# Reordering the ends of the layer normalisations in a two-layer hybrid decoder kernel: transposes in four banks, the layers written out, the last step in halves, angle tables later, the store in parts

## The chip, the core and the metric

The kernel runs on one core of a Trainium2 chip (trn2). The metric is the device time of one execution in microseconds, as the median of several runs. The engines are named as in the profile: PE is TensorE (PEld its weight loads), DVE is VectorE, ACT is ScalarE, POOL is GpSimd, SP is the engine that issues most DMAs. A name with a small q at its end (DVEq, SPq) is an engine's queue: its branches, register instructions and DMA issues.

## The reference

Two post-norm decoder layers over 256 tokens of width 1024, in float32. What matters here is where the normalised stream `x` is made and who reads it:

```python
h = layer_norm(x, ln_in_g, ln_in_b)
for l in range(DEPTH):                       # DEPTH = 2
    # token mixing: one input projection, MLA and NSA attention, gates, output projection
    c_q, c_kv, k_r, n_q, n_kv, n_gate, m_gate = split(h @ w_in[l])
    ...
    h = layer_norm(ALPHA * h + mixed, ln1_g[l], ln1_b[l])
    # channel mixing: PEER retrieval over 128*128 single-neuron experts
    q = h @ peer_w_query[l]; ...; a = h @ expert_u.T (dense in the kernel); ...
    h = layer_norm(ALPHA * h + peer(h), ln2_g[l], ln2_b[l])
```

So the stream is normalised five times in a run: once for the input, and twice in each layer. The rotary embeddings need the cosine and sine of position times frequency, one small table for the whole run.

## The kernel before

**Tiles.** The tokens are two groups `tt` = 0, 1 of 128 rows; `xs` holds the stream, 128 partitions x 2 x 1024. All weights stream from memory as 512 KB tiles of 128 x 1024 into a ring of four slots (`raw`). Each is split in two parts whose sum is the full number: ACT writes the high part (`split_hi`, L443), DVE writes what is left (`split_lo`, L701), and every product is three matmuls (low x high, high x low, high x high: L1206 to L1208 where the result is wanted transposed, L1217 where tokens are rows). A slot is free again when PE has used its tile, and only then SP issues the next load into it (L367). Tile n+3 is split while tile n is multiplied (`AHEAD` = 3). A layer has 68 front tiles (8 for the latent projections, 52 more up to the output projection, 8 for the PEER query), then 128 tiles of expert keys (the "u" stage, L1515) and, after a stage that builds the gates from one-hot rows (L1539), 128 tiles of expert values (the "v" stage, L1554).

**A normalisation.** DVE does for each token group, one after the other: add the wide sum out of PSUM (L1021), statistics (two of L715, then L717), the variance (L721), subtract the mean and multiply by the gain (L723), and, when POOL has made the inverse root (L408), the last step (L728), which multiplies by it and adds the bias. L728 is one instruction of 128 x 1024; it adds 1 to the semaphore `x_ready`.

**After it.** The next matmuls want `x` transposed and split as well. PE transposes 128 x 128 blocks, four to a PSUM bank (L1235), in the order g = 0..3: g = 0, 1 are the halves of token group 0, g = 2, 3 those of group 1. The PSUM tensor `tr` has two banks, so g = 2 must wait until the low part of g = 0 has been read out (`tr_free`, L1194). For each g ACT writes the high part (L476) and then DVE the low part (L779). When DVE has done all four (`xT_written`), PE starts on the first tile. PE, ACT and DVE each follow a fixed order of instructions. On ACT the high parts come after the splits of three weight tiles; on DVE, at the first layer's start and at the second's, the low part of weight tile 0 comes first, then the four low parts of `x`, then those of tiles 1 and 2. After the first normalisation of a layer the low part of the first query tile is put between L723 and L728 of token group 1 (`meanwhile`).

**The start.** DVE first computes the angles (L736 to L751, 13 instructions, on a tile `ang` that overlays the latents), then the input normalisation, then copies the sines and cosines that ACT has made (L465, L466) into the tables (L761 to L768), and then enters the loop over layers.

**The loop.** On each engine the two layers are one loop of hardware instructions (`Fori(0, DEPTH)`, L369, L412, L468, L772, L1228) around inner loops; addresses and the values that waits compare with are computed from the loop register.

**The end.** When both groups are ready SP stores all of `xs`, 1 MB, with one DMA (L375).

## Time and profile before

| | before |
|---|---|
| median of 3 runs | 2387.64 us (2386.96 to 2390.41) |
| the profiled execution | 2391.61 us, of which 2390.0 us are the span |
| PE busy | 2191.5 us (92%) |
| PE weight load busy | 1976.3 us (83%) |
| DVE busy | 1579.1 us (66%) |
| ACT busy | 1190.1 us (50%) |
| DMA | 353 MB, mean 148 GB/s |

The busy shares are averages over the stages. In 40 equal slices of the span (one digit is the busy share in tenths, a 9 is 90% or more; PEclk is the clock that TensorE was granted, in tenths of its 2.4 GHz):

```profile
PE   6989989999996699999988898999999967999997
DVE  5546567777769955555556466577777698555555
PEclk9989999999999999999989899999999999999999
```

The slices where PE falls below 9 are the start, the attention stages, the gate stages (slices 13 and 33), the places where one normalisation ends and the next product begins, and the end.

### The profile page before, as it was taken

To read this page: it belongs to the slowest core of one execution; us is meant where nothing else is said; L and a number is where in the kernel's file an instruction comes from. 1 tells how busy PE (TensorE), PEld (TensorE's weight loads), DVE (VectorE), ACT (ScalarE), POOL (GpSimd) and SP (SyncE) were. 2 spreads that over 40 slices of the span, in tenths; PEclk is the share of its full clock that TensorE was granted. 3 is DMA by queue.
4 is the path that set the end of the run, shared out by engine and by line. 5 is a ranking of instruction groups with operands and counts; after the bars stand their busy time and mean duration, and the time that the engine had idled before them with its cause. 6 is when DMAs were issued, how large, how long until landed. Compare 5 with 4: busy or idle time off the path is not lost.

```text
span 2390.0 us, 43583 instructions
## 1 busy us (share of the span) xinstructions
PE 2191.5 (92%) x14072; PEld 1976.3 (83%) x14072; DVE 1579.1 (66%) x3274; ACT 1190.1 (50%) x2060; POOL 32.0 (1%) x48
## 2 busy tenths in 40 slices
PE   6989989999996699999988898999999967999997
PEld 6878779999995588788777877899999955887886
DVE  5546567777769955555556466577777698555555
ACT  4435444554457645455434354455445676554553
POOL 1000000000000000000000000000000000000000
PEclk9989999999999999999989899999999999999999
DMA  4622335555550055665546114355555400556554
GB/s 143 221 70 71 128 128 184 181 181 183 184 178 8 0 173 191 198 193 193 174 131 208 53 63 159 123 180 182 183 184 179 164 0 9 193 193 202 193 193 140
DMA packets 96307, 353.44 MB, mean 148 GB/s; under 512 B 11056, under 2 KB 11088, under 8 KB 95856
## 3 DMA queue, kind: packets, MB, share of 16 engines
q1 hardware_dynamic: 94032, 341.90, 43.7%
q0 software_dynamic: 2208, 10.66, 1.3%
q8 instruction: 40, 0.66, 0.1%
q14 instruction: 27, 0.22, 0.0%
HBM read 351.47 MB, written 1.05 MB: 147 GB/s over the span
## 4 chain that ended last, share of the span: by engine, by line
PE 61%; issue 25%; DVE 7%; DMA 2%; ACT 2%; DVEq 1%; POOL 1%; SPq 0%; ACTq 0%; POOLq 0%
PE wide L1217 14%; PE acc L1206 13%; PE acc L1208 13%; PE acc L1207 13%; DVE hot_j L1126 3%; DMA raw<-in_front 2%; PE acc L1536 2%; DVE big L1146 1%; PE wide L1392 1%; PE acc L1345 1%; PE tr L1317 1%; DVE hot_i L1134 1%; DVEq L1126 1%; ACT hi L443 1%; PE acc L1363 0%
## 5 line engine op out<-in xcount | busy, mean ns | idle before, releaser
L701 DVE TENSOR_TENSOR lo<-raw,hi 128x1024 fp32r<-128x1024 f32 x648 | 792.5, 1224 | 602.1 <-ACT hi L443 596.4
L443 ACT ACTIVATE hi<-raw 128x1024 fp32r<-128x1024 f32 x648 | 686.7, 1060 | 557.6 <-DMA raw<-in_peer_v 356.0
L1206 PE MATMUL acc<-xT_hi,lo 128*128 128x256 f32 x2560 | 733.9, 287 | 8.9 <-DVE xT_lo L779 7.3
L1207 PE MATMUL acc<-xT_lo,hi 128*128 128x256 f32 x2560 | 731.1, 286 | 0.0
L1208 PE MATMUL acc<-xT_hi,hi 128*128 128x256 f32 x2560 | 731.0, 286 | 0.0
L1206 PEld LDWEIGHTS acc<-xT_hi,lo 128*128 128x128 f32 x2560 | 499.0, 195 | 11.8 <-issue 9.8
L1207 PEld LDWEIGHTS acc<-xT_lo,hi 128*128 128x128 f32 x2560 | 499.0, 195 | 0.2
L1208 PEld LDWEIGHTS acc<-xT_hi,hi 128*128 128x128 f32 x2560 | 498.3, 195 | 0.0
L1217 PE MATMUL wide<-hi,w_lo 128*128 128x512 f32 x1024 | 318.5, 392 | 12.3 <-DVE w_lo L1163 12.3
L1217 PE MATMUL wide<-hi,w_hi 128*128 128x512 f32 x1024 | 317.3, 391 | 0.0
L1217 PE MATMUL wide<-lo,w_hi 128*128 128x512 f32 x1024 | 317.2, 391 | 0.0
L627 ACT ACTIVATE big<-acc 128x256 f32 (+1 forms) x256 | 98.2, 384 | 306.6 <-PE acc L1208 306.3
L1217 PEld LDWEIGHTS wide<-hi,w_lo 128*128 128x128 f32 x1024 | 193.4, 190 | 55.0 <-DVE lo L701 11.1
L1536 PE MATMUL acc<-hot_j,hot_i 128*128 128x128 f32 x1024 | 159.0, 305 | 79.5 <-DVE big L1146 50.2
L1217 PEld LDWEIGHTS wide<-lo,w_hi 128*128 128x128 f32 x1024 | 193.3, 189 | 40.6
L1217 PEld LDWEIGHTS wide<-hi,w_hi 128*128 128x128 f32 x1024 | 193.4, 189 | 40.5
L1536 PEld LDWEIGHTS acc<-hot_j,hot_i 128*128 128x128 f32 x1024 | 136.0, 208 | 102.4 <-issue 87.8
L652 ACT ACTIVATE hot_i<-iota,picksT 128x128 f32<-128x128 f32 x384 | 121.6, 388 | 49.7 <-PE acc L1536 49.7
L1126 DVE TENSOR_SCALAR hot_j<-iota,picksT 128x128 f32<-128x128 f32 x512 | 141.4, 340 | 0.4 <-issue 0.2
L680 ACT ACTIVATE w_hi<-big 128x256 fp32r (+1 forms) x256 | 102.2, 401 | 13.1 <-DVE big L1146 13.1
L1163 DVE TENSOR_TENSOR w_lo<-big,w_hi 128x256 fp32r<-128x256 f32 x256 | 106.9, 418 | 1.1 <-ACT w_hi L680 1.1
L1146 DVE TENSOR_TENSOR big<-acc,big 128x512 f32 (+1 forms) x128 | 87.4, 684 | 5.3 <-PE acc L1536 5.1
(234 smaller groups left out, 1730.0 us busy)
## 6 DMA issues: line engine op xcount, KB each, us to landing
raw<-in_peer_u SPq DMA_DIRECT2D x256, 512.0 KB, 3.3
raw<-in_peer_v SPq DMA_DIRECT2D x256, 512.0 KB, 3.3
raw<-in_front SPq DMA_DIRECT2D x136, 512.0 KB, 3.4
ln_par<-in_ln POOLq DMA_DIRECT2D x10, 512.0 KB, 5.3
w<-in_cmp_w POOLq DMA_DIRECT2D x2, 2048.0 KB, 10.3
xs<-in_x SPq DMA_DIRECT2D x2, 512.0 KB, 7.3
keys<-in_sub_keys POOLq DMA_DIRECT2D x2, 512.0 KB, 3.6
out<-xs SPq DMA_DIRECT2D x1, 1024.0 KB, 3.9
```

The source lines that it names most:

```text
L443: nc.scalar.activation(hi[:, s], raw[:, s], ACT.Identity).then_inc(hi_done, 1)
L652: ins = nc.scalar.activation(hot_i[:, e, r], iota[:], ACT.Abs, bias=picksT[:, 0, bass.ds(tok, 1)], scale=-1.0)
L680: nc.scalar.activation(w_hi[:, s].rearrange("p (g t) -> p g t", t=TB), big[:, i + c // JB, :, c % JB], ACT.Identity).then_inc(w_hi_done, 1)
L701: nc.vector.tensor_tensor(lo[:, s], raw[:, s], hi[:, s].bitcast(F32), ALU.subtract).then_inc(lo_done, 1)
L1126: ins = nc.vector.tensor_scalar(hot_j[:, e % HOTS, r], iota[:], picksT[:, 1, bass.ds(tok, 1)], picksT[:, 2, bass.ds(tok, 1)], ALU.is_equal ...
L1146: nc.vector.tensor_tensor(part, acc[:, e % 2].rearrange("p (t a j) -> p a j t", t=TB, j=JB), part, ALU.mult).then_inc(acc_read[e % 2], 1)
L1163: nc.vector.tensor_tensor(w_lo[:, s].rearrange("p (g t) -> p g t", t=TB), big[:, i + c // JB, :, c % JB], part, ALU.subtract).then_inc(w_l ...
L1206: mm(dst, lo[:, s, c], xh[:, k], start=k == 0, stop=False)
L1207: mm(dst, hi[:, s, c], xl[:, k], start=False, stop=False)
L1208: ins = mm(dst, hi[:, s, c], xh[:, k], start=False, stop=k == DK - 1)
L1217: ins = mm(wide[:, tt, 512 * h:512 * h + width], a[:, tok], w[:, s, off:off + width], start=first and k == 0, stop=last and k == 2)
L1536: ins = mm(acc[:, e % 2, r * P:(r + 1) * P], hot_i[:, e, r], hot_j[:, e, r], start=True, stop=True)
```

## The change

On all engines the loop over the two layers becomes a Python loop, so that the code of the second layer stands behind that of the first and there is no branch back. The last step of each normalisation is issued as two instructions of 512 columns, each with its own signal. The transposes of token group 1 go to two banks of `wide`, which nobody uses at that time, with semaphores of their own (`wide_x_ready`, `wide_x_read`). Low parts of `x` move: that of g = 0 between L723 and the last step of group 1 (for the second normalisation of a layer it is the first work of the next layer that goes there; not at the start), and that of g = 1 ahead of the low part of the first weight tile. On ACT only one weight tile (at the start and the second layer's start; two of the three at the first normalisation's end) is split before the high parts of group 0. The angles are computed after the splits of tiles 1 and 2 of the first layer, ACT's sines after all its high parts, and the tables are filled after the latent projections; `ang` moves to another place. The store is three DMAs: group 0, and two halves of group 1.

```diff
@@ SP
-            with sp.Fori(0, DEPTH) as l:
+            for l in range(DEPTH):
...
-            sp.wait_ge(x_ready, TT * (1 + 2 * DEPTH))
-            sp.dma_start(out, xs[:]).then_inc(stored, 16)
-            sp.wait_ge(stored, 16)
+            last = 2 * TT * (2 * DEPTH)
+            sp.wait_ge(x_ready, last + 2)
+            sp.dma_start(out[:, 0], xs[:, 0]).then_inc(stored, 16)
+            for c in range(2):
+                sp.wait_ge(x_ready, last + 2 + c + 1)
+                sp.dma_start(out[:, 1, 512 * c:512 * c + 512], xs[:, 1, 512 * c:512 * c + 512]).then_inc(stored, 16)
+            sp.wait_ge(stored, 48)
@@ ACT
-            act.wait_ge(angles_ready, 1)
-            nc.scalar.activation(ang[:, 2], ang[:, 0], ACT.Sin).then_inc(sines_ready, 1)
-            nc.scalar.activation(ang[:, 3], ang[:, 1], ACT.Sin).then_inc(sines_ready, 1)
-            with act.Fori(0, DEPTH) as l:
+            for l in range(DEPTH):
                 warm_up(ACT.Gelu, l * 2 + 1)
-                for n in range(AHEAD):
-                    split_hi(l, 0, n)
...
+                split_hi(l, 0, 0)
                 transposed_hi(X_XT, 0, xT_part)
+                for n in range(1, AHEAD):
+                    split_hi(l, 0, n)
+                transposed_hi(X_XT, 1, xT_part)
+                if l == 0:
+                    act.wait_ge(angles_ready, 1)
+                    nc.scalar.activation(ang[:, 2], ang[:, 0], ACT.Sin).then_inc(sines_ready, 1)
+                    nc.scalar.activation(ang[:, 3], ang[:, 1], ACT.Sin).then_inc(sines_ready, 1)
...
-                for n in range(T_OUT, T_PQ):
+                for n in range(T_OUT, T_PQ - 1):
                     tile_step(l, n)
-                transposed_hi(X_XT2, 4, xT_part)
+                transposed_hi(X_XT2, 0, xT_part)
+                tile_step(l, T_PQ - 1)
+                transposed_hi(X_XT2, 1, xT_part)
@@ DVE
-                nc.vector.scalar_tensor_tensor(out=xs[:, tt], in0=xs[:, tt], scalar=rstd[:, tt:tt + 1],
-                                               in1=ln_par[:, 1], op0=ALU.mult, op1=ALU.add).then_inc(x_ready, 1)
+                for c in range(2):
+                    half = slice(512 * c, 512 * c + 512)
+                    nc.vector.scalar_tensor_tensor(out=xs[:, tt, half], in0=xs[:, tt, half], scalar=rstd[:, tt:tt + 1],
+                                                   in1=ln_par[:, 1, half], op0=ALU.mult, op1=ALU.add).then_inc(x_ready, 1)
...
-            (the angles, L734 to L751)
             chain = Steps(dve, ln_step, 0, TT * 4)
             for tt in range(TT):
                 ...
                 normalise(tt, tt, 32, chain)
-            (wait for the sines, the tables, L758 to L769)
-            with dve.Fori(0, DEPTH) as l:
-                split_lo(l, 0, 0)
+            for l in range(DEPTH):
...
-                transposed_lo(X_XT, 0, x_part(xT_hi), x_part(xT_lo))
+                if l == 0:
+                    transposed_lo(l, 0, 0)
+                transposed_lo(l, 0, 1)
+                split_lo(l, 0, 0)
+                transposed_lo(l, 0, 2)
+                transposed_lo(l, 0, 3)
                 split_lo(l, 0, 1)
                 split_lo(l, 0, 2)
+                if l == 0:
+                    (the angles)
                 dve.wait_ge(small_loaded, l * 48 + 48)
                 for c in range(N_LAT):
                     ...
+                if l == 0:
+                    (wait for the sines, the tables)
...
-                add_and_norm(0, T_PQ - 1, W_OUT, R_LN1, l * 64 + 64, lambda: tile_step(l, T_PQ - AHEAD))
-                transposed_lo(X_XT2, 4, x_part(xT_hi), x_part(xT_lo))
+                add_and_norm(0, T_PQ - 1, W_OUT, R_LN1, l * 64 + 64, lambda: transposed_lo(l, 1, 0))
+                transposed_lo(l, 1, 1)
+                tile_step(l, T_PQ - AHEAD)
+                transposed_lo(l, 1, 2)
+                transposed_lo(l, 1, 3)
...
-                add_and_norm(1, NT - 1, W_V, R_LN2, l * 64 + 96)
+                add_and_norm(1, NT - 1, W_V, R_LN2, l * 64 + 96,
+                             (lambda: transposed_lo(l + 1, 0, 0)) if l + 1 < DEPTH else None)
@@ PE
-            with pe_.Fori(0, DEPTH) as l:
-                def transpose_x(first, nth):
+            for l in range(DEPTH):
+                def transpose_x(first, nth, use):
                     for g in range(4):
                         tt, cg = divmod(g, 2)
-                        pe_.wait_ge(x_ready, nth + tt + 1)
-                        tr_free(l, first + g)
+                        pe_.wait_ge(x_ready, 4 * nth + g + 1)
+                        if tt == 0:
+                            tr_free(l, first + cg)
+                            dst, done = tr[:, cg], tr_ready
+                        else:
+                            if cg == 0:
+                                pe_.wait_ge(wide_read[0], OPEN + l * NWIDE + use)
+                            dst, done = wide[:, 0, 512 * cg:512 * cg + 512], wide_x_ready
                         for c in range(4):
-                            ins = nc.tensor.transpose(tr[:, (first + g) % 2, c * P:(c + 1) * P],
+                            ins = nc.tensor.transpose(dst[:, c * P:(c + 1) * P],
                                                       xs[:, tt, (4 * cg + c) * P:(4 * cg + c + 1) * P], ident[:])
-                        ins.then_inc(tr_ready, 1)
+                        ins.then_inc(done, 1)
```

## Rows read from the trace of the kernel before

**Rows 1.** The page: the last chain by engine, then the view of waits (us in total, times, longest).

```profile
PE 61%; issue 25%; DVE 7%; DMA 2%; ACT 2%; DVEq 1%; POOL 1%; SPq 0%; ACTq 0%; POOLq 0%
...
PE tr L1235 <- DVE xT_lo L779: 28.0, 4, 8.7
```

**Rows 2.** The timeline, the start: start and duration in us, engine, line, operation, [idle before].

```profile
5.76 0.17 DVE L736 CAST pos_f<-pos_i 128x2 f32<-128x2 int32 x1 [5.76 <-DMA freq<-in_freq]
6.37 1.28 ACT L465 ACT_TABLE_LOAD   x1
8.81 1.41 DVE L715 BATCH_NORM_STATS2 stats<-xs 128x6 f32<-128x512 f32 x2
17.49 1.28 DVE L728 SCALAR_TENSOR_TENSOR xs<-xs,rstd,ln_par 128x1024 f32<-128x1024 f32 x1 [0.52 <-POOL rstd L408]
20.65 1.23 DVE L701 TENSOR_TENSOR lo<-raw,hi 128x1024 fp32r<-128x1024 f32 x1 [0.22 <-DVE sin_n L768]
21.79 1.28 DVE L779 TENSOR_TENSOR xT_lo<-tr,xT_hi 128x512 fp32r<-128x512 f32 x2
26.20 0.58 PE L1206 MATMUL acc<-xT_hi,lo 128*128 128x256 f32 x1 [1.70 <-DVE xT_lo L779]
30.91 0.39 ACT L488 ACTIVATE sq<-acc 128x256 f32<-128x256 f32 x1 [5.78 <-PE acc L1208]
```

**Rows 3.** The timeline's issue of the input's two loads, and their time to landing.

```profile
2.12 0.90 SPq L359 DMA_DIRECT2D xs<-in_x  x2
...
DMA to landing us min/median/max: 6.2/7.3/8.4
```

**Rows 4.** The timeline where the first normalisation of layer 0 ends.

```profile
304.44 1.28 DVE L723 SCALAR_TENSOR_TENSOR xs<-xs,mv,ln_par 128x1024 f32<-128x1024 f32 x1
305.84 1.23 DVE L701 TENSOR_TENSOR lo<-raw,hi 128x1024 fp32r<-128x1024 f32 x1
308.92 1.97 PE L1235 MATMUL tr<-ident,xs 128*128 128x128 f32 x8 [6.37 <-DVE xT_lo L779]
311.55 0.69 DVE L779 TENSOR_TENSOR xT_lo<-tr,xT_hi 128x512 fp32r<-128x512 f32 x1 [0.16 <-ACT xT_hi L476]
312.82 0.58 PE L1206 MATMUL acc<-xT_hi,lo 128*128 128x256 f32 x1 [1.94 <-DVE xT_lo L779]
```

**Rows 5.** The timeline where layer 0 ends and layer 1 begins.

```profile
1194.30 1.06 ACT L443 ACTIVATE hi<-raw 128x1024 fp32r<-128x1024 f32 x1 [5.77 <-DMA raw<-in_front]
1195.23 1.09 PE L1235 MATMUL tr<-ident,xs 128*128 128x128 f32 x8 [1.01 <-DVE xs L728]
1198.13 1.28 DVE L723 SCALAR_TENSOR_TENSOR xs<-xs,mv,ln_par 128x1024 f32<-128x1024 f32 x1
1203.17 1.23 DVE L701 TENSOR_TENSOR lo<-raw,hi 128x1024 fp32r<-128x1024 f32 x1 [2.03 <-issue]
1208.71 0.58 PE L1206 MATMUL acc<-xT_hi,lo 128*128 128x256 f32 x1 [1.70 <-DVE xT_lo L779]
```

**Rows 6.** One line's instructions: the branches of DVE's layer loop and gate loop.

```profile
L772 DVEq COMPARE_BRANCH  x2: 43/53/63, 1199.9 to 2384.5; - x2
...
L1151 DVEq COMPARE_BRANCH  x30: 50/56/56, 725.6 to 2014.7; - x30
```

**Rows 7.** Busy time by stretch: us, then PE, PEld, DVE, ACT, POOL, granted clock, DMA.

```profile
1195.00:1208.70 13.70, 3.06 (x16) 2.42 (x16) 9.58 (x14) 4.64 (x7) 3.13 (x4) 0.58 0.28 93
1208.70:1214.00 5.30, 5.29 (x25) 5.29 (x25) 1.94 (x2) 0.00 (x0) 0.00 (x0) 0.50 0.00 0
```

**Rows 8.** The timeline: the end.

```profile
2384.39 1.28 DVE L728 SCALAR_TENSOR_TENSOR xs<-xs,rstd,ln_par 128x1024 f32<-128x1024 f32 x1 [0.44 <-POOL rstd L408]
2385.70 0.35 SPq L375 DMA_DIRECT2D out<-xs  x1
```

**Rows 9.** DMA issues by line: KB of each, median us from issue to landing.

```profile
out<-xs SPq DMA_DIRECT2D x1, 1024.0 KB, 3.9
...
pos_i<-in_positions SPq DMA_DIRECT2D x1, 1.0 KB, 1.8
```

## What the change will do

> **What bounds the kernel now.** I read the page first. PE is busy 92% of the span, and of the chain that ended last it holds 61% and "issue", which in the expert stages is PE going from one matmul to the next, another 25% [rows 1]. So time can be won only where PE stands still, or by making PE's work shorter; the change doesn't touch a matmul of the products. The view of waits then shows which standstills belong to the normalisations: the transposes wait 28.0 us in all for the low parts of `x` [rows 1], and the timeline shows the five places. They are the start [rows 2], the first normalisation of either layer [rows 4] (one of two, with the same rows and the same distances), the change from layer 0 to layer 1 [rows 5], and the end [rows 8]. At each the reader should see one chain: DVE's last step (L728), PE's transposes, ACT's high part, DVE's low part, the first product. DVE is on it nearly all the time, so what counts is the order of DVE's instructions, and what stands between them that PE doesn't need yet. Between these places PE runs against slots, loads and DVE in the same relative order before and after, so a shift of PE's start moves all that follows.
>
> **Lengths used.** Low part of `x`: two in 1.28 us, so 0.60 from start to start and 0.68 for the last [rows 2]. Low part of a weight tile: 20.65 to 21.79, 1.14 from start to start [rows 2]. The half step isn't in the trace: the whole takes 1.28 us for 1024 columns [rows 2], so a half takes between 0.64 and, with a cost of its own like that of a low part of 512 columns, 0.70; I take 0.63 from start to start, which makes two of them 0.05 longer than the one. From the end of the last low part (311.55 + 0.69 = 312.24) to the first product 0.58 us pass after a first normalisation [rows 4]; PE's idle time before it is 1.94 there and 1.70 at the two layer starts [rows 2, 4, 5], 0.24 less behind the same transposes, so I take 0.34 there.
>
> **First normalisation of a layer, twice.** Before, DVE puts the low part of the query tile behind L723, at 305.84; PE starts at 312.82 [rows 4], 6.98 us later. After, from 305.84: low part g = 0 (0.60), two halves (0.63 + 0.63), low part g = 1 (0.60), the weight tile (1.14), low parts g = 2 and 3 (0.60 + 0.68), 4.88 us; and 0.58 more is 311.30. Gain 1.5 us, in two layers 3.0. What must be in time: g = 2 is transposed from the end of the first half, 0.60 + 0.68 = 1.28 after 305.84, plus 0.15 to start. Before, g = 3's low part began 311.55 - 308.92 = 2.63 us after PE began with g = 2 [rows 4]; so it can begin at 1.43 + 2.63 = 4.06, and its turn comes at 4.20. It is just hidden, by 0.14 us; if PE or ACT is later by more, the chain grows by that, and I allow 0.3 a place. The wait for `wide_read` is over by then, since L1021 of group 0 is the first thing that DVE does. On ACT one weight tile moves behind the high parts of group 0; what is queued behind the new order is that tile alone, which the third product needs.
>
> **From layer 0 to layer 1.** L723 ends at 1198.13 + 1.28 = 1199.41, and DVE's next begins 0.12 after it, as in rows 4: 1199.53. The same chain of 4.88 and 0.34 gives 1204.75, against 1208.71 [rows 5]. Gain 4.0 us. Half of it is the 2.03 us "issue" before L701 [rows 5], when DVE waits for nothing; DVE's branch back stands at 1199.9 [rows 6], 3.2 us before that L701. With the layers written out there is none. For the low part of g = 0 DVE now waits on ACT, behind the split of tile 0, which ends at 1194.30 + 1.06 = 1195.36, and PE's transposes from 1195.23 on [rows 5]: both are over 3 us before their turn. Queued behind that wait on DVE is only the last step itself; if tile 0 came 3 us later, it would cost what goes beyond.
>
> The branch row is where the Trainium skill bears on this ("Runtime: NRT & Kernel Launch", Instruction fetch mechanics): it says that a taken branch out of the two pages at hand stops the engine until the page is fetched, and that straight code is fetched ahead. The gap at the outer branch agrees with it. By that rule the 2.03 us go entirely; were they a cost of fresh code instead, this gain would be 2.0.
>
> **The start.** The angles stand first on DVE, 5.76 to the statistics at 8.81, 3.1 us [rows 2], but they hide behind the input's load: issued at 2.12, landed 6.2 us later at 8.3 [rows 3]. So moving them gives between 0 and 0.5; I take 0.4, as the gains' load may be late too. L728 of group 1 then starts at 17.49 - 0.4 + 0.05 = 17.14 [rows 2]. Behind it, after: two halves 1.26, low parts g = 0 and 1 1.20, the weight tile 1.14, g = 2 and 3 1.28, and 0.34: 5.22, so 22.36 against 26.20 [rows 2]. Gain 3.8 us. Of it some 1.9 us are the tables (18.77 to 20.65 [rows 2]), the rest the two banks. Where they go: the angles run on DVE after the splits of tiles 1 and 2, from 22.4 - 0.3 - 0.1 + 2.3 = 24.3 to 27.4, and ACT's sines until 28.0. ACT is queued behind them with the first latent result, which comes 30.91 - 26.20 = 4.7 after PE's start [rows 2], at 27.1. It is 0.9 late. PE wants that bank again one product later, at 30.0, and reading it takes about 1.3: 29.3, hidden by 0.7. If ACT must load a table once more (1.28, as at 6.37 [rows 2]) between sine and square, 0.6 show. So 0 to 0.6; I take 0. The eight table copies land after the latents, where DVE waits for PE's sums and nothing of layer 0 wants the tables; 0, or up to 1.9 without that cover.
>
> **The end.** Before: last step 2384.39, store at 2385.70, 3.9 us to landing, 2389.6 [rows 8, 9]. After: the last half ends at 2385.70 and its 256 KB are issued at 2385.75, with group 0 long gone. The nearest rows are 1.8 us for 1 KB and 3.9 for 1024 KB [rows 9]; on the line between them 256 KB take 2.3, with 0.1 for the half before it in the queue: 2388.15. Gain 1.4; the ends are 2.0 (1.8 us to land) and -0.1 (3.9).
>
> The Trainium skill ("DMA: Bandwidth & Descriptors", Anatomy of one DMA) puts a DMA at 2.0 us and the bytes by 436 GB/s, 4.4 for the store, where the row has 3.9; by its slope the end would gain 1.8.
>
> **Written-out layers otherwise.** Register instructions fall away on every queue, but the engines' rows show them under running work; 0, or a few tenths gained at each chain. SP and POOL issue the same DMAs in the same order.
>
> **The sum.** 3.8 + 3.0 + 4.0 + 1.4 = 12.2 us. The profiled execution took 2391.61 (span 2390.0 and 1.6 around it), so it would take 2379.4; it lies 4.0 above the median of the runs, 2387.64, and there the sum gives 2375.4. The error of each part: start -1 to +0.5, first normalisations -0.6 to +0.4, layer change -2 to +0.5, end -1.5 to +0.6. After each place PE runs at half of its clock for some time: behind 1208.71 for 5.3 us at a granted 0.50 [rows 7], which costs 2.65 us. That this stretch is longer or shorter changes a place by 1 us or so, either way.
>
> **The rivals.** (a) The clock. PE stood from 1196.3 to 1208.7 with eight transposes in it, and had fallen to 1.2 GHz (mean 0.58 [rows 7]). After, the stand is 4 us shorter and split by the transposes. If the clock stays up at the three inner places, each gives up to 2.65 more: 2367.5. Against it: the stand is still 8 us and the transposes are two microseconds of work. 0.08. (b) A new wait takes a part back: DVE is still held at the layer change (2.0), ACT behind the sines (0.6) and high parts late (0.3 at four places): 2.0 + 0.6 + 1.2 = 3.8, so 2379.2. 0.10. (c) The change doesn't do what it says: what follows PE's start is bound by loads that don't start earlier, and the four inner gains are given back before the next place; only the end is left, 2386.2. Against it: the slots' loads are issued when PE frees them, so they move with PE. 0.06. (d) Slower: the code of the second layer lies elsewhere, and if its gate loop no longer stays within what DVE holds, each branch back costs DVE what the outer one does, 3.1 us. There are 30 passes in two layers [rows 6], 15 in the new code, and DVE has no idle time in that stage, so +46: 2422. It decides from 0.8 us a pass on. Against it: in 30 passes before, the branch row is a short one with work on both sides, and the body is no longer than before. 0.04.
>
> **How the numbers follow.** My forecast, all parts as summed, has 0.72: 2375.4. Its own range is 2372.5 to 2378.5. To hold 8 in 10 I go a little into (a) and over (b): 2371 to 2381. About 0.2% (4.8 us) is what a measurement here can tell from no change. Faster by more: the forecast, (a) and (b), 0.89 with a rest for bad luck taken off; within: (c) and that rest, 0.07; slower: (d), 0.04.
>
> **What would show it.** In the profile after: the first product at 22.4; from the start of L723 of group 1 to the first product 6.9 us at the first normalisations (8.4 before) and 6.6 at the layer change (10.6 before); no "issue" idle on DVE at the layer change; the last store issued 1.3 to 1.4 us after the last step's start and landing in 2.3 to 2.6. Wrong would be: ACT idle until L751 with PE waiting for `acc` behind it, DVE waiting for ACT's L476 for longer than 0.3 us, or a change in the length of the u, gate or v stages, which the sum holds at nothing.

## The result and the profile after

The changed kernel takes 2373.72 us (median of 4 runs, 2373.4 to 2375.43) against 2387.3 us for the kernel before in the same session (4 runs, 2385.62 to 2390.41). The ratio is 0.9943, with an interval of 0.9926 to 0.9960: a gain of 13.6 us, between 9.6 and 17.7. In a second session it was 0.9946 (0.9931 to 0.9961), 12.9 us. The forecast was 12.2 us and 2375.4 us. The profiled execution took 2373.94 us, of which 2371.9 are the span. One run of a kernel below took 3560.56 us at a granted clock of 0.555 and is in no time or ratio here.

The page of the kernel after: busy time by engine, and the last chain by engine.

```profile
PE 2190.9 (92%) x14072; PEld 1974.7 (83%) x14072; DVE 1577.1 (66%) x3284; ACT 1187.8 (50%) x2059; POOL 31.6 (1%) x48
...
PE 81%; DVE 10%; issue 3%; DMA 2%; ACT 2%; DVEq 1%; POOL 0%; POOLq 0%; ACTq 0%; SPq 0%
```

PE does the same 14072 matmuls in 2190.9 us (2191.5 before); only its standstills became shorter. That the chain gives "issue" 3% where [rows 1] had 25%, and PE 81% for 61%, is a matter of how the chain is followed through back-to-back matmuls: their sum is 84% for 86%.

The timeline of the kernel after, the start (start and duration in us, engine, line, operation, [idle before]). The lines have other numbers than before: L730 is the statistics, L738 the mean step (subtract the mean, multiply by the gain; L723 before), L745 the last step, now in halves (L728 before), L768 a low part of `x`, L716 that of a weight tile, L1267 the transposes, L1231 the first of the three products, L496 and L501 ACT's sine and first latent result.

```profile
9.17 1.42 DVE L730 BATCH_NORM_STATS2 stats<-xs 128x6 f32<-128x512 f32 x2 [9.17 <-DMA xs<-in_x]
...
17.87 1.41 DVE L745 SCALAR_TENSOR_TENSOR xs<-xs,rstd,ln_par 128x512 f32<-128x512 f32 x2 [0.52 <-POOL rstd L414]
...
20.40 1.21 DVE L716 TENSOR_TENSOR lo<-raw,hi 128x1024 fp32r<-128x1024 f32 x1
...
21.53 1.28 DVE L768 TENSOR_TENSOR xT_lo<-wide,xT_hi 128x512 fp32r<-128x512 f32 x2
...
23.02 0.55 PE L1231 MATMUL acc<-xT_hi,lo 128*128 128x256 f32 x1 [2.37 <-issue]
...
28.15 0.28 ACT L496 ACTIVATE ang<-ang 128x96 f32<-128x96 f32 x1 [5.57 <-DVE ang L812]
...
28.51 0.36 ACT L501 ACTIVATE sq<-acc 128x256 f32<-128x256 f32 x1
```

The reader should see that nothing stands between L745 at 17.87 and the last L768 but low parts: the sines' eight copies of [rows 2] are gone. The first product comes at 23.02, not at 26.20. ACT waits 5.57 us for the angles, and the first latent result stands behind that wait; PE doesn't wait for it.

The timeline where the first normalisation of layer 0 ends, to be laid beside [rows 4].

```profile
300.68 1.27 DVE L738 SCALAR_TENSOR_TENSOR xs<-xs,mv,ln_par 128x1024 f32<-128x1024 f32 x1
...
302.59 1.40 DVE L745 SCALAR_TENSOR_TENSOR xs<-xs,rstd,ln_par 128x512 f32<-128x512 f32 x2
...
303.39 1.97 PE L1267 MATMUL wide<-ident,xs 128*128 128x128 f32 x8 [5.05 <-DVE xs L745]
303.92 0.68 DVE L768 TENSOR_TENSOR xT_lo<-tr,xT_hi 128x512 fp32r<-128x512 f32 x1
304.52 1.21 DVE L716 TENSOR_TENSOR lo<-raw,hi 128x1024 fp32r<-128x1024 f32 x1
...
305.65 1.28 DVE L768 TENSOR_TENSOR xT_lo<-wide,xT_hi 128x512 fp32r<-128x512 f32 x2
...
307.53 0.58 PE L1231 MATMUL acc<-xT_hi,lo 128*128 128x256 f32 x1 [2.17 <-DVE xT_lo L768]
```

PE's transposes begin behind the first half (303.39), while DVE is in the second, and wait for a low part no more. DVE goes from 300.68 to 306.93 without a gap: the two last low parts stand as one row of two, so ACT's high part of g = 3 was in time. From L738 of token group 1 to the first product ("the distance" below): 6.85 us, before 8.38.

The same where layer 0 ends and layer 1 begins, to be laid beside [rows 5].

```profile
1191.80 1.28 DVE L738 SCALAR_TENSOR_TENSOR xs<-xs,mv,ln_par 128x1024 f32<-128x1024 f32 x1
...
1193.72 1.40 DVE L745 SCALAR_TENSOR_TENSOR xs<-xs,rstd,ln_par 128x512 f32<-128x512 f32 x2
...
1195.64 1.21 DVE L716 TENSOR_TENSOR lo<-raw,hi 128x1024 fp32r<-128x1024 f32 x1
...
1198.26 0.55 PE L1231 MATMUL acc<-xT_hi,lo 128*128 128x256 f32 x1 [1.78 <-issue]
```

The 2.03 us "issue" ahead of the weight tile's low part is gone: L716 begins 3.84 us after L738, where L701 began 5.04 after L723. First product 6.46 us after L738, before 10.58.

Behind it, the windows view (us, then busy us of PE, PEld, DVE, ACT and POOL, granted clock, DMA share), beside [rows 7].

```profile
1198.20:1204.00 5.80, 5.74 (x27) 5.77 (x28) 2.12 (x2) 0.25 (x1) 0.00 (x0) 0.51 0.01 3
1204.00:1210.00 6.00, 6.00 (x52) 6.00 (x52) 3.42 (x4) 3.50 (x8) 0.00 (x0) 1.00 0.51 175
```

PE still works at 1.2 GHz (a granted 0.51) for nearly all of the first 5.8 us and does 27 matmuls in them; at 2.4 GHz it does 52 in 6.0.

The end: the timeline, and the DMA issues (KB of each, median us to landing), beside [rows 8, 9].

```profile
2367.94 1.41 DVE L745 SCALAR_TENSOR_TENSOR xs<-xs,rstd,ln_par 128x512 f32<-128x512 f32 x2 [0.52 <-POOL rstd L414]
2368.72 0.99 SPq L381 DMA_DIRECT2D out<-xs  x2
...
out<-xs SPq DMA_DIRECT2D x1, 512.0 KB, 2.7
out<-xs SPq DMA_DIRECT2D x2, 256.0 KB, 2.2
```

The first half's store is issued before the second half is computed, and a store of 256 KB lands in 2.2 us, one of 1024 KB took 3.9.

### The profile page after: what moved, and what is told of

It reads as the page before. It is cut to its first block, busy times and chain, and to the rows that moved or that the text cites. A ratio compares the mean times of both kernels' runs of the same rounds, so it can differ in the third digit from the quotient of the medians.

```text
span 2371.9 us, 42588 instructions
## 1 busy us (share of the span) xinstructions
PE 2190.9 (92%) x14072; PEld 1974.7 (83%) x14072; DVE 1577.1 (66%) x3284; ACT 1187.8 (50%) x2059; POOL 31.6 (1%) x48
## 4 chain that ended last, share of the span: by engine, by line
PE 81%; DVE 10%; issue 3%; DMA 2%; ACT 2%; DVEq 1%; POOL 0%; POOLq 0%; ACTq 0%; SPq 0%
PE wide L1242 32%; PE acc L1231 13%; PE acc L1232 13%; PE acc L1233 13%; DVE hot_j L1150 3%; DVE big L1170 2%; PE acc L1569 1%; DMA raw<-in_front 1%; PE wide L1425 1%; PE acc L1378 1%; PE tr L1350 1%; DVE lo L716 1%; DVE hot_i L1158 1%; DMA raw<-in_peer_v 1%; PE acc L1500 1%
## 5 line engine op out<-in xcount | busy, mean ns | idle before, releaser
L716 DVE TENSOR_TENSOR lo<-raw,hi 128x1024 fp32r<-128x1024 f32 x648 | 792.0, 1223 | 585.3 <-ACT hi L449 583.7
L1231 PE MATMUL acc<-xT_hi,lo 128*128 128x256 f32 x2560 | 734.0, 287 | 9.9 <-DVE xT_lo L768 4.3
L1231 PEld LDWEIGHTS acc<-xT_hi,lo 128*128 128x128 f32 x2560 | 499.2, 195 | 13.1 <-issue 10.9
```

Of the source, the lines that this page charges most:

```text
L716: nc.vector.tensor_tensor(lo[:, s], raw[:, s], hi[:, s].bitcast(F32), ALU.subtract).then_inc(lo_done, 1)
L1231: mm(dst, lo[:, s, c], xh[:, k], start=k == 0, stop=False)
```

## The experiments

Runs of one kernel scatter by 5 us to either side, so a part that is worth 1 us doesn't show in a ratio. Each experiment is therefore read twice: in its ratio to the kernel before (runs of the same session; an interval holds the true ratio 95 times in 100), and in the distance from the start of L738 of group 1 (L723 before) to the first product, which repeats between two executions of one kernel to 0.1 us, and to 0.25 at the layer change of the kernel before. The whole table first (distances in us at the four places, then the median time with the number of runs):

| kernel | start | 1st norm., layer 0 | layer change | 1st norm., layer 1 | time, us (runs) | ratio (interval) |
|---|---|---|---|---|---|---|
| before (profile shown above) | 10.50 | 8.38 | 10.58 | 8.38 | 2387.3 (4) | 1 |
| before again | 10.50 | 8.41 | 10.33 | 8.37 | 2389.42 (12) | 0.9999 (0.9990 to 1.0009) |
| layers written out only | 10.14 | 8.32 | 8.36 | 8.23 | 2389.3 (12) | 1.0002 (0.9990 to 1.0014) |
| the same, again | 10.14 | 8.22 | 8.36 | 8.22 | 2389.08 (11) | 1.0003 (0.9990 to 1.0016) |
| after | 6.95 | 6.85 | 6.46 | 6.84 | 2373.72 (4) | 0.9943 (0.9926 to 0.9960) |
| after again | 6.95 | 6.86 | 6.46 | 6.85 | 2377.5 (6) | 0.9946 (0.9931 to 0.9961) |
| two banks and late low parts | 8.60 | 8.53 | 8.59 | 8.50 | 2384.27 (12) | 0.9982 (0.9970 to 0.9994) |
| two banks | 7.46 | 7.12 | 6.72 | 7.11 | 2379.32 (10) | 0.9967 (0.9950 to 0.9983) |
| late low parts | 6.95 | 7.18 | 6.95 | 7.18 | 2377.6 (8) | 0.9956 (0.9940 to 0.9972) |
| whole last step | 6.85 | 7.17 | 6.78 | 7.17 | 2377.02 (6) | 0.9950 (0.9933 to 0.9968) |
| angles and tables early | 8.77 | 6.86 | 6.46 | 6.85 | 2378.73 (7) | 0.9960 (0.9946 to 0.9975) |
| high x high first | 5.30 | 5.42 | 5.42 | 5.42 | 2370.62 (4) | 0.9927 (0.9905 to 0.9948) |
| PE filled | 6.95 | 6.86 | 6.46 | 6.94 | 2376.94 (7) | 0.9963 (0.9946 to 0.9981) |
| both of these | 5.18 | 4.77 | 4.77 | 4.77 | 2366.43 (4) | 0.9921 (0.9899 to 0.9944) |

**The kernel before, again.** The same code, for the scatter.

> The kernel before, once more, for a second profile. The first two profiles lie 18.1 us apart in span (2390.0 and 2371.9) while the chains at the five normalisation ends account for 11.5 us of it (start 3.2, first normalisations 1.4 and 1.4, layer change 4.0, end 1.5). Theory A, the rest is chance (clock stretches and late loads of one execution): this profile's span is nearer to 2386 and its chains have the same lengths as in the first profile (L723 of group 1 to the first product 8.4 us at the first normalisations, 10.6 at the layer change). Theory B, the rest is a cost that the kernel before always has: span again 2389 to 2391, with layer 1's front stage some 4 us longer than in the changed kernel, as in the first profile. Time 2387, within 0.1% of the kernel before.

Ratio 0.9999, and the same distances. What follows is measured against this.

**The layers written out, and nothing else.** The kernel before, with on each engine

```diff
-            with dve.Fori(0, DEPTH) as l:
+            for l in range(DEPTH):
```

> The kernel before with nothing changed but the five layer loops, which become Python loops. Theory A (only DVE's branch back costs): the 2.03 us of 'issue' before L701 at the layer change are gone, L723 of group 1 to the first product falls there from 10.6 to 8.5 us, all other chains stay, time 2385.3 (2.0 less). Theory B (register instructions on all queues cost as well): the chains at the first normalisations get shorter too, by 0.1 to 0.3 us each, and the front stages by 1 to 4 us: time 2381 to 2384. Theory C (fresh code costs): a new gap of 1 us or more stands somewhere in layer 1, time 2386 to 2388.

The timeline at the layer change of this kernel:

```profile
1195.10 1.27 DVE L723 SCALAR_TENSOR_TENSOR xs<-xs,mv,ln_par 128x1024 f32<-128x1024 f32 x1
...
1198.09 1.22 DVE L701 TENSOR_TENSOR lo<-raw,hi 128x1024 fp32r<-128x1024 f32 x1
...
1203.46 0.55 PE L1206 MATMUL acc<-xT_hi,lo 128*128 128x256 f32 x1 [1.46 <-DVE xT_lo L779]
```

L701 follows 2.99 us after L723, 5.04 before, and it has no idle time in front of it; the distance to the product fell from 10.58 (10.33 in the other execution) to 8.36. In the trace before, DVE's queue has nothing between the branch, over at 1200.00, and a register instruction at 1203.05. So the gap was the branch's, all of it. The Trainium skill ("Runtime: NRT & Kernel Launch", Instruction fetch mechanics) has a taken branch out of the pages at hand wait for its page; by that rule the gap goes with the branch, and the trace agrees.

But the time didn't follow: 1.0002 (0.9990 to 1.0014), where a gain of 2.1 us would be 0.9991. The same kernel in another session:

> The kernel before with written-out layers, once more: its first profile had the chain at the layer change 2.2 us shorter (8.36 us from L723 to the first product, 10.58 and 10.33 before), but its times showed 1.0002 of the kernel before (0.9990 to 1.0014). Theory A (chance): now 0.9990 or less, 2385. Theory B (written-out code costs elsewhere what it gives at the change): 1.000 to 1.001 again.

1.0003 (0.9990 to 1.0016), and 8.36 again. Each interval just holds the 2.1 us; both centres are against them. The windows view of one stretch, the small score matmuls behind the PEER query in layer 1, first of the kernel before, then of the written-out one.

```profile
1525.40:1532.60 7.20, 6.69 (x64) 6.07 (x64) 5.10 (x21) 4.92 (x9) 0.00 (x0) 1.00 0.20 75
```

```profile
1517.00:1526.70 9.70, 9.47 (x64) 9.31 (x64) 6.80 (x28) 5.13 (x8) 0.00 (x0) 0.63 0.17 57
1526.70:1530.00 3.30, 3.30 (x17) 3.08 (x17) 2.56 (x8) 0.60 (x1) 0.00 (x0) 0.55 0.00 0
```

The same 64 matmuls take 9.7 us at a granted 0.63 instead of 7.2 at 1.00, and the stretch goes on at 0.55 behind them, so that the part from the first product of the PEER query to the last of the u stage is 406.6 us long, 402.5 to 403.1 in the kernel before. Each profile has two such places. In the two profiles of this kernel three of four are slow, in the two of the kernel before none of four, in the ten profiles of all other kernels here, whose layers are written out too, 5 of 20 ("after" 0 of 2, "after again" 1). One such place costs more than the layer change gives. The clocks of all runs say that this isn't chance: the mean granted clock of this kernel is 0.9628 (12 runs) and 0.9622 (11), that of the kernel before in the same sessions 0.9648 (29) and 0.9651 (20), with errors of 0.0003 to 0.0009. A difference of 0.0020 to 0.0029 is 5 to 7 us of 2388 if PE has work all the while (an estimate), more than the 2.1; so the gain was most likely lost in the clock. Nor is it written-out code as such: the changed kernel, written out as well, has 0.9653 in its second session. What lowers the clock of this one kernel no run here shows.

Something else came with the written-out layers, at the start. SP issues the first weight load at 3.25 to 3.26 us in the twelve profiles of written-out kernels, at 3.65 in the two of the kernel before. The input's first load then takes 6.9 to 7.3 us to land, before 5.8 and 6.2. That the earlier weight loads slow the input's was not tested.

**After again, and after with two of its parts undone together.** First the changed kernel itself:

> The changed kernel once more, as the partner of these runs and for a second profile. 2373.7 within 1 us if the first measurement was typical; chains of 6.85 us at the first normalisations and 6.5 at the layer change again, whatever the span. If the clock stretch behind each of them (5.5 us in the first profile of it, 3.7 to 5.3 in the kernel before) is chance, it differs here; if the shorter stand makes it longer, it is 5.5 again at all places.

0.9946, and distances that repeat to 0.01 us. Then only two banks again (a transposition of group 1 waits until the bank of group 0 is read; it still goes to `wide`, but no earlier than with two banks), and the low parts of group 0 back behind the last step; at the two layer starts too the weight tile's low part stands first again (cut):

```diff
+                            pe_.wait_ge(tr_read[cg], OPEN + l * (NTR // 2) + first // 2 + 1)
...
-                add_and_norm(0, T_PQ - 1, W_OUT, R_LN1, l * 64 + 64, lambda: transposed_lo(l, 1, 0))
-                transposed_lo(l, 1, 1)
-                tile_step(l, T_PQ - AHEAD)
+                add_and_norm(0, T_PQ - 1, W_OUT, R_LN1, l * 64 + 64, lambda: tile_step(l, T_PQ - AHEAD))
+                transposed_lo(l, 1, 0)
+                transposed_lo(l, 1, 1)
```

> The changed kernel with two of its parts taken back together: the transposes of token group 1 wait for the low parts of group 0 as they did with two banks, and the low part of the first weight tile goes ahead of the low parts of x again (no low part of x stands before the last step). Theory A (what PE waits for at these places is the chain of low parts): the first normalisations go back to about 8.4 us from L723 to the first product (6.85 in the changed kernel), layer change 8.5, the start 1.5 us later; 4 x 1.6 = 6.4 us more than the changed kernel, 2380. Theory B (DVE's total work sets it, the order does not matter): within 1 us of the changed kernel, 2374.5.

Its timeline at the first normalisation of layer 0:

```profile
302.92 1.41 DVE L745 SCALAR_TENSOR_TENSOR xs<-xs,rstd,ln_par 128x512 f32<-128x512 f32 x2
304.25 1.28 DVE L768 TENSOR_TENSOR xT_lo<-tr,xT_hi 128x512 fp32r<-128x512 f32 x2
305.08 1.94 PE L1266 MATMUL wide<-ident,xs 128*128 128x128 f32 x8 [6.95 <-DVE xT_lo L768]
...
306.83 0.69 DVE L768 TENSOR_TENSOR xT_lo<-wide,xT_hi 128x512 fp32r<-128x512 f32 x1 [1.30 <-ACT xT_hi L481]
```

The old chain is back: PE waits for a low part (it starts 2.16 us after the last step does, 0.80 in the change), and DVE then waits 1.30 us for ACT. Distance 8.53 for 6.85; over the four places 7.1 us in all; and the ratio falls back from 0.9946 to 0.9982, 8.6 us. The intervals don't meet. That these two parts together carry most of the gain is shown both ways, by the starts and by the time.

**One of the two at a time.** Two banks alone, with the low parts where the change has them:

> The changed kernel, in which only the gain of the four banks is taken back: the transposes of token group 1 wait until the low parts of group 0 have been read. With both this and the order of the low parts taken back the chain from L723 of group 1 to the first product was 8.5 us, against 6.85. Theory A (the two parts do the same thing twice: since the low parts of group 0 are done early, the banks are free in time): 6.9 to 7.3 us at the first normalisations and the layer change 6.5 to 6.9, the start 0.3 to 0.6 later; time within 1.5 us of the changed kernel. Theory B (each part gives its share, about half of the 1.7): 7.7 us.

and the low parts back alone, with four banks:

> The changed kernel, in which only the order of DVE's low parts is taken back: the first weight tile's low part first, then the four of x, and nothing but that tile before the last step; four banks stay. Theory A (the parts stand in for each other): DVE's work in the chain is the same, 4.9 us, and the transposes begin 0.5 later at the first normalisations, so 7.2 to 7.4 us from L723 of group 1 to the first product there; at the layer change nothing fills the wait for the root: 6.9 to 7.1. Theory B (half each): 7.7 us.

The timeline at the same place, of the first and then of the second:

```profile
307.30 1.09 PE L1268 MATMUL wide<-ident,xs 128*128 128x128 f32 x4 [0.24 <-DVE xT_lo L768]
...
309.05 0.69 DVE L768 TENSOR_TENSOR xT_lo<-wide,xT_hi 128x512 fp32r<-128x512 f32 x1 [0.17 <-ACT xT_hi L481]
```

```profile
304.10 1.97 PE L1265 MATMUL wide<-ident,xs 128*128 128x128 f32 x8 [5.59 <-DVE xs L745]
304.63 1.28 DVE L768 TENSOR_TENSOR xT_lo<-tr,xT_hi 128x512 fp32r<-128x512 f32 x2
```

With two banks PE loses only 0.24 us before g = 3, because the low parts are early; with late low parts PE loses nothing, because it has a bank. The distance grows by 0.27 and 0.33 us at the first normalisations, where both undone cost 1.68. At the layer change it is 0.26 and 0.49, against 2.13. So each part stands in for the other: neither is worth half of the sum, and one alone would have brought nearly all of it. Only at the start do two banks cost more (0.51), since there the low part of g = 0 has no place ahead of the last step. The ratios (0.9967 and 0.9956) are too wide to see 0.3 us a place.

**The last step in one.**

```diff
-                for c in range(2):
-                    half = slice(512 * c, 512 * c + 512)
-                    nc.vector.scalar_tensor_tensor(out=xs[:, tt, half], in0=xs[:, tt, half], scalar=rstd[:, tt:tt + 1],
-                                                   in1=ln_par[:, 1, half], op0=ALU.mult, op1=ALU.add).then_inc(x_ready, 1)
+                nc.vector.scalar_tensor_tensor(out=xs[:, tt], in0=xs[:, tt], scalar=rstd[:, tt:tt + 1],
+                                               in1=ln_par[:, 1], op0=ALU.mult, op1=ALU.add).then_inc(x_ready, 2)
```

> The changed kernel with the last step as one instruction of 1024 columns again. Two halves take 1.41 us in the changed kernel and the whole took 1.28. Theory A (the halves are worth it only in group 1): group 0 gets 0.13 us faster, from group 1's L723 on PE gets the first half 0.6 later and the last low part waits for ACT: 0.4 to 0.5 us longer, so 7.3 us instead of 6.85, net +0.2 to +0.3 us a place, and +0.3 at the end (both last stores at once). Sum about 1.3 us more than the changed kernel, not to be seen in the time. Theory B (the halves cost more than they give): chain 6.8 us or less.

```profile
303.29 1.27 DVE L744 SCALAR_TENSOR_TENSOR xs<-xs,rstd,ln_par 128x1024 f32<-128x1024 f32 x1
304.48 0.68 DVE L772 TENSOR_TENSOR xT_lo<-tr,xT_hi 128x512 fp32r<-128x512 f32 x1
304.62 1.97 PE L1271 MATMUL wide<-ident,xs 128*128 128x128 f32 x8 [5.15 <-DVE xs L744]
```

The whole step takes 1.19 us from start to start, the two halves 1.33 (302.59 to 303.92 above). PE's transposes start 1.33 us behind the step's start and not 0.80, ACT's high parts are late by that, and the distance is 7.17 for 6.85. Against it the mean step of group 1 comes 0.10 us sooner after that of group 0 (6.17 for 6.27), and from L738 of group 0 to the product the halves win 0.22 (13.12 for 13.34). The ratio, 0.9950, can't tell it from 0.9946.

**The angles and the tables back in their old places**, ahead of the input normalisation and behind it, and ACT's sines ahead of its layers, with all else as in the change. On ACT, and likewise on DVE:

```diff
+            act.wait_ge(angles_ready, 1)
+            nc.scalar.activation(ang[:, 2], ang[:, 0], ACT.Sin).then_inc(sines_ready, 1)
+            nc.scalar.activation(ang[:, 3], ang[:, 1], ACT.Sin).then_inc(sines_ready, 1)
...
-                if l == 0:
-                    act.wait_ge(angles_ready, 1)
-                    nc.scalar.activation(ang[:, 2], ang[:, 0], ACT.Sin).then_inc(sines_ready, 1)
-                    nc.scalar.activation(ang[:, 3], ang[:, 1], ACT.Sin).then_inc(sines_ready, 1)
```

> The changed kernel with the angles ahead of the input normalisation and the tables behind it again. In the changed kernel the statistics begin when the input has landed, at 9.2 us in its profile, and ACT sits behind the sines for 1.1 us at most. Theory A: only the table copies count, 1.9 us in front of the low parts (group 1's L723 to the first product 8.9 instead of 6.95), the angles hide behind the load as before; first product at 24.9 to 25.5. Theory B: moving the angles was worth something too: statistics later than the landing by more than 0.3 us.

```profile
9.25 1.43 DVE L729 BATCH_NORM_STATS2 stats<-xs 128x6 f32<-128x512 f32 x2 [0.30 <-DMA xs<-in_x]
...
19.28 0.21 DVE L777 COPY cos_m<-ang 128x32 f32<-128x32 f32 x1
...
21.09 1.29 DVE L797 TENSOR_TENSOR xT_lo<-tr,xT_hi 128x512 fp32r<-128x512 f32 x2
...
24.92 0.55 PE L1226 MATMUL acc<-xT_hi,lo 128*128 128x256 f32 x1 [4.20 <-issue]
```

The eight copies from 19.28 to 21.09 are on the path: 1.82 us of the distance. The angles are not: with all 13 instructions ahead of it DVE still waits 0.30 us for the input, and begins its statistics at 9.25, against 8.86 to 9.31 in the nine profiles with the angles behind.

**What is left at these places.** Two things still stood behind the change: PE's start waits for the last low part, and PE then works at 1.2 GHz. Three kernels ask whether they can be had. In the first, the first tile multiplies in another order, and the query tiles are written out for it; otherwise it is the changed kernel: 8 products high x high, 8 low part of the weights x high, and only then, behind the waits for `x`'s low parts, 8 high x low part of `x`.

```diff
+            def opening_tile(l, nth, first, q, s, bank):
...
+                pe_.wait_ge(tr_hi, l * 8 + (nth - 2 * l) * 4 + 4)
+                pe_.wait_ge(hi_done, l * NT + q * SLOTS + s + 1)
+                for k, c in enumerate(parts):
+                    mm(dst, hi[:, s, c], xT_hi[:, k], start=k == 0, stop=False)
+                tile_ready(l, q, s)
+                for k, c in enumerate(parts):
+                    mm(dst, lo[:, s, c], xT_hi[:, k], start=False, stop=False)
+                for b in range(2):
+                    pe_.wait_ge(tr_read[b], OPEN + l * (NTR // 2) + first // 2 + 1)
+                pe_.wait_ge(wide_x_read, 2 * nth + 2)
+                for k, c in enumerate(parts):
+                    ins = mm(dst, hi[:, s, c], xT_lo[:, k], start=False, stop=k == DK - 1)
...
-                xT_written(X_XT, 2 * l)
-                for c in range(N_LAT):
+                acc_free(l, A_LAT)
+                opening_tile(l, 2 * l, X_XT, 0, 0, 0)
+                for c in range(1, N_LAT):
```

> The changed kernel with another order of PE's matmuls in the first tile behind each normalisation: first all eight high x high products, which need only ACT's high parts, then the eight with the tile's low part, then the eight with the low parts of x (and the eight query tiles written out instead of a hardware loop). Theory A (PE waits for DVE's last low part, and only for that): PE starts when ACT has written the fourth high part, 5.5 us from group 1's L723 at the first normalisations instead of 6.85, and never waits again in the tile; 1.2 to 1.4 us at each of four places, 2372.5 where the changed kernel had 2377.5 in the same session. Theory B (DVE's low parts still set the end of the tile): PE starts early but stands inside the tile, and the second tile begins less than 0.5 us earlier.

The distance is 5.42 us at the three inner places, 1.43 less than in the change at the first normalisations, 1.04 less at the layer change, 1.65 less at the start, and nowhere does PE wait inside the tile. The timeline at the first normalisation of layer 0:

```profile
310.42 2.05 PE L1243 MATMUL acc<-xT_hi,hi 128*128 128x256 f32 x8 [0.73 <-issue]
```

Ratio 0.9927 (0.9905 to 0.9948), an interval that overlaps that of the changed kernel: the earlier start is shown in the trace, not in the time.

In the second, PE is given something to do between the transposes of group 0 and those of group 1 (and ahead of the first ones at the start): 20 matmuls of 512 columns on the identity, whose sums nobody reads.

```diff
+                            def fill(n):
+                                for _ in range(n):
+                                    mm(acc[:, 1], ident_r[:], ident_r[:].unsqueeze(1).broadcast_to([P, 4, P]), start=True, stop=True)
+                            if g == 2:
+                                fill(6 if nth == 0 else 20)
```

> The changed kernel with matmuls that compute nothing in PE's waits: 20 of 128x512 (identity by identity, into a free bank) between the transposes of group 0 and those of group 1 at each of the three inner places, at the start 16 before the first transposes and 6 between. Theory A (the clock fell because PE stood still: granted 0.5 for 5.2 to 5.7 us behind each place): the granted clock stays 1.0 from the last product to the first, eight transposes take 1.1 instead of 1.97 us, the first tile 2.9 instead of 5.3: 2.4 us at each of four places, and some 0.5 more where ACT is waited for; 9 to 10 us less than the changed kernel, 2367. Theory B (filling doesn't hold the clock): the 20 take 0.43 us each, end 4 us late, and each place loses 4 us: 2389.

And the third has both.

> Both of the two before. If A holds in both: the first tile starts 5.0 us after group 1's L723 and takes 2.9: 4 x (1.3 + 2.4 + 0.6) = 16 us less than the changed kernel, about 2361. If they overlap (a shorter stand leaves less for the clock to lose): 12 us.

The windows view at the first normalisation of layer 0, of the filled kernel. The transposes of group 1 run from 303.17 to 304.49 and the first product starts at 307.31:

```profile
303.20:306.00 2.80, 1.28 (x8) 0.81 (x8) 2.80 (x4) 2.05 (x3) 0.00 (x0) 1.00 0.00 0
306.00:307.30 1.30, 0.00 (x0) 0.00 (x0) 1.30 (x3) 0.63 (x2) 0.00 (x0) 0.53 0.00 0
...
307.30:312.00 4.70, 4.68 (x22) 4.69 (x23) 1.67 (x2) 0.00 (x0) 0.00 (x0) 0.50 0.01 3
```

and of the kernel with both, with its timeline:

```profile
301.60:303.70 2.10, 1.31 (x8) 0.86 (x9) 2.10 (x4) 1.26 (x3) 0.00 (x0) 1.00 0.00 0
303.70:308.00 4.30, 4.29 (x36) 4.30 (x37) 3.77 (x5) 2.47 (x4) 0.00 (x0) 1.00 0.03 7
...
296.36 4.81 PE L1279 MATMUL acc<-ident_r 128*128 128x512 f32 x20
...
303.71 1.18 PE L1243 MATMUL acc<-xT_hi,hi 128*128 128x256 f32 x8 [0.73 <-issue]
```

The fill keeps the clock at 1.00 through itself and through the transposes (1.32 us for eight, 1.97 in the change). It isn't enough: in the standstill of 2.83 us before the product the clock falls, and the first tile takes 5.28 us, as in the change; so it does in layer 1 (2.91 us, then 5.27). At the layer change of the same kernel the standstill is 2.43 us, and the clock falls only 1.0 us into the first tile, which takes 4.42 us for 5.25:

```profile
1195.93 0.36 PE L1231 MATMUL acc<-xT_hi,lo 128*128 128x256 f32 x1 [2.43 <-issue]
...
1197.15 0.41 PE L1231 MATMUL acc<-xT_hi,lo 128*128 128x256 f32 x1
```

The first eight matmuls follow each other at 0.12 us, the next at 0.21. The ratio, 0.9963, is no better than the changed kernel's; 2367 us were expected and 2376.94 came. With the other order the standstill is 0.73 us, the clock stays at 1.00, and the first tile takes 2.94, 2.94 and 2.95 us at the three inner places (4.90 at the start). This kernel has the lowest median: 2366.43 us (2361 were expected), 0.9921 (0.9899 to 0.9944), 18.9 us under the kernel before; its profile's span is 2358.0. Its interval touches that of the reordered kernel without fill (0.9927), so the ratio of the two is not told apart; the tile's 2.95 for 5.28 us is in the trace. Against the changed kernel (0.9946 and 0.9943) it lies 5 to 6 us lower, with intervals that overlap.

## Why the prediction held, and where it was off

**What bounds the kernel.** PE's starts, with DVE's chain ahead of them. This was right: the undone pair of parts moved both the starts (7.1 us) and the time (8.6).

**First normalisations, 1.5 us each.** Measured 1.37 and 1.40, counted from L1021 of group 0. The chain behind L723 gained 1.53 (8.38 to 6.85), within 0.1 of the working; what was mis-sized is the half step. I took 0.63 us from start to start; two of them take 1.33, not 1.26, and group 0 pays for them too, which the sum counted at the start alone. L738 of group 0 to L738 of group 1 is 6.27 us for 6.07; with the whole step it is 6.17, so 0.10 is the halves, and with the layers written out alone 6.14. That g = 3 would be "just hidden by 0.14" was right: the last two low parts follow without a gap, while in the kernels with two banks, with late low parts or with a whole step a gap of 0.16 or 0.17 us is there again.

**Layer change, 4.0.** Measured 4.04, and 6.46 us from the mean step to the product for 6.6. Its halves: 2.0 to 2.2 are the branch, and 1.9 the order. The wait of the low part of g = 0 on ACT cost nothing.

**Start, 3.8.** Measured 3.2: first product at 23.02, not 22.4. The last step of group 1 was worked out at 17.14 and began at 17.87: 0.73 late. Of that 0.4 is the gain that the angles were to give, 0.1 the halves of group 0, and the rest goes with later landings: the input landed at 9.17, not at 8.3 as in [rows 3], and then the mean step of group 0 waited 0.40 us for the gains' load. In the kernel before, the statistics began at 8.81 without waiting for the input (8.40 in its other profile). With the angles in front the statistics began at 9.25, without them at 8.86 to 9.31, so moving them gave nothing. Two steps failed: the 0.4 for the angles, and that the landing would stay where it was; with the layers written out alone the statistics already begin at 9.17 and 9.18. The order behind it gained what it should: L745 to the product 5.15, worked out 5.22. The tables were sized right, at 1.8 for 1.9. ACT's sines came at 28.15 and 28.34, the square at 28.51, with no table load between; PE, done with its first tile at 27.4, never waited for the bank.

**End, 1.4.** Measured 1.42 from the start of the last product to the end (11.61 to 10.19), though the halves cost some 0.1 of it. The store in parts was not undone by itself. A store of 256 KB lands in 2.2 us, where the line between [rows 9] gave 2.3. The Trainium skill ("DMA: Bandwidth & Descriptors", Anatomy of one DMA) has 2.0 us and the bytes by 436 GB/s: 2.6 for 256 KB and 3.2 for 512 KB. It gives this for DMAs that GpSimd issues, which the prediction didn't say; these are issued by SP. The rows have 2.2 and 2.7; the measurement decides, and its slope is near the page's while the fixed part is some 0.4 to 0.5 us less.

**The sum.** 3.2 + 1.4 + 1.4 + 4.0 + 1.4 = 11.4 us by the trace, 12.2 predicted, 13.6 and 12.9 by the runs with 4 to either side. So the trace accounts for a little less than the runs show, and that the forecast lies between the two is partly luck. The two profiled spans differ by 18.1. Of the 6.7 beyond the sum 6.0 lie in one stretch, from the first product of layer 1 to the mean step of its first normalisation (276.3 to 270.3 us), where 46 us were at 1.2 GHz before and 36 after; in the changed kernel's other profile, whose span is 2378.5, it is 46 again and the stretch 274.7. In the whole span 154 us are at 1.2 GHz in the first profile, 168 in the other, 172 and 170 in the two before.

**The rivals.** (a) The clock stays up: no; 1.2 GHz for 5.5 to 5.6 us behind each inner place (4.1 to 5.7 in the other profile, 3.7 to 5.5 in the two before), so the shorter standstill saved none of it. Even with PE filled before the transposes it didn't stay up, as long as 2.4 to 2.9 us of standstill were left. (b) A new wait: none of the three places named has one. (c) Absorbed by loads: the stages behind keep their length within some 3 us (first to last product of query and u 402.5 and 403.1 us before, 403.4 in both layers after; v 357.8 and 355.2 before, 356.2 and 356.4 after), and the time moved. (d) The gate loop refetched: no; from the last product of u to the first of v 120.6 us pass in both layers, before 121.1. What I held at nothing and can't confirm as nothing is writing out the layers: its own gain is there in the trace and not in its time, with a lower granted clock (0.9628 and 0.9622 for 0.9648 and 0.9651) and a later input.

## What to carry to other kernels

Where an engine's start hangs on a chain over three engines, write down start-to-start times from the last common event; the sum was good to 0.1 us a place behind the mean step, and the errors were a cost of cutting an instruction in two (0.14 us for the pair) that was mis-sized and not counted everywhere, and the landing of a load. Value two parts that shorten the same chain together and each without the other: here each was worth 0.3 us on top of the other and both 1.7. With split products, multiply first what is ready first (high x high): that started PE 1.4 us earlier at a first normalisation, and only with it did filling PE's standstill keep its clock. In the time neither is told apart from the changed kernel. And when a part's gain is in the trace but not in the time, compare the granted clocks of all the runs before calling it chance.

## What the runs showed of the hardware

- A fill doesn't save the clock if a short standstill follows: 4.82 us of matmuls, 1.32 of transposes at a granted 1.00, and the clock was at 0.5 after a standstill of 2.83 us; at the layer change it held through 2.43 us and fell 1.0 us into the tile (4.42 us). After one of 0.73 it stayed at 1.00 and the tile took 2.95 us instead of 5.28.
- At the first product of all the view of the granted clock reads 1.00 from 22.98 to 30.0, yet the first 15 matmuls follow each other at 0.21 us as they do at 1.2 GHz (0.12 at 2.4 GHz), and the first tile takes 4.39 us. The trace has no record of the clock before 26.30 us, where one of 1.00 begins, and the pitch changes at 26.34; where there is no record the view prints 1.00. In the filled kernel the records begin at 9.11 and give 0.50 from 19.35 to 26.17: there the first eight transposes, at 13.46, take 1.32 us (1.94 without fill), the clock falls again before the product, and the tile takes 4.42.
- A taken branch back over the whole layer cost DVE 2.03 us of visible standstill at the layer change (1.78 in the other profile), 3.05 us from the branch to the queue's next instruction; ACT's square behind its sine needed no table load.
